# Attention scores of the batch after next put between the turns and the outputs, with the early tiles, query turns and columns' sums reordered

## The chip, the cores and the metric

The kernel runs on one core of one Trainium2 chip. The metric is the device time of one execution in microseconds (us); the number before is the median of 3 runs. A matmul runs on TensorE (PE in the rows), element-wise work on VectorE (DVE), ScalarE (ACT) and GpSimd (POOL); SyncE (SP) issues the loads.

## What is computed

The reference is one block of a first kind, followed by a block of two layers of a second kind, on 512 tokens of width 1024, batch 1, in float32. Cut to what matters here:

```python
# first block: mixer (retention + sparse attention), then a gated feed-forward
h = x + rms_norm(concat([retention(...), dsa_attention(...)]) @ w_out, g_post)
h = h + rms_norm(swiglu_conv(rms_norm(h, g)) @ w_down, g_post)
# second block, layer 0: gated linear attention; layer 1: attention over shared keys
mods = einsum('bd,lde->lbe', silu(c), ada_w) + ada_b      # shift, scale, gate per layer and part
x = x + gate * mixer(rms_norm_2(x, g) * (1 + scale) + shift)
x = x + gate * swiglu(rms_norm_2(x, g) * (1 + scale) + shift, w_in, w_out)
# attention in both blocks: softmax(scale * q @ k.T + mask) @ v, 64 wide per head, tokens in 4 blocks of 128
```

The first block's attention (name `dsa`) has 32 units, one for each of 4 token blocks and 8 heads. The second block's (name `nsa`) has 128 units: 4 token blocks, 16 heads, 2 branches. A unit of token block t reads (t+1)*128 keys, so its rows are n = 128, 256, 384 or 512 wide. `dsa` goes from narrow to wide, `nsa` from wide to narrow. Ahead of `nsa` there is a small attention over 31 compressed keys (`cmp`).

## The kernel before

Each engine has one hand-written program, and semaphores tie them together. An engine takes its instructions strictly in the order in which they are written, so a wait holds everything that stands behind it. Results of TensorE land in the 8 banks of PSUM (`ps`). `open_bank(key)` makes TensorE wait until the last reader of the bank has freed it, `filled(engine, key)` makes a reader wait for the result, `evacuated(engine, key)` waits until it was read. The banks are given out by a plan that runs before the programs are written (`plan_bank`, `plan_attention`).

**Attention** (`attention` of the TensorE program, L2446, with `att_scores`, L2436) goes in batches of four units. For a batch there are these steps: *scores* (L2443, four products q*k into banks 0 to 3, unit i into bank i%4, in two pairs); on VectorE the *logits* (L1770, `logit`: reads the score bank, adds the mask, finds the largest; this frees the bank); on ScalarE the *exponential* (L1134); on TensorE the *turns* (L2461, 128x128 transposes into banks 4 to 6); *copies* of the turned tiles to SBUF, for widths over 256 by ScalarE for even units (L1167) and by VectorE for odd ones (L1794), for the narrow widths two units at a time (L1164, L1791); on TensorE the *outputs* (L2487, bank 7). After every second batch TensorE also turns the finished outputs back (L2472, the key "B"). In step j TensorE does the scores of batch j, the turns of batch j-1, B where due, the outputs of batch j-1.

VectorE's program for step j (`attention` of the VectorE part) is: logits of units 4j, 4j+1, 4j+2; the copies of the turned units 4j-3 and 4j-1 of batch j-1; the logit of unit 4j+3; then `finish` where due. The change leaves this order as it is.

**Norms.** `norm(i)` on TensorE turns the normalised rows of x, one token tile t at a time, into 8 banks ("xT", i, kt). `keep_busy` puts in transposes of the identity whose result nobody reads; `BUSY` says how many stand ahead of each tile. ScalarE (L1014, L1016) and VectorE then read the banks. Ahead of norm(2) and norm(4) TensorE makes the *columns' sums*: `ada_sums`, L2368, sums over partitions of 2 and 4 accumulated rows of `mods`, four one-column products each, with 4 `keep_busy` ahead of each group. They land in a bank of their own, and VectorE's `ada_columns` (L1626, L1636) makes shifts and gains of them.

**Output products.** `out_parts` and the loop over `out_weight` split each piece of the output weight into a high part (ScalarE, L1028) and a low part (VectorE, L1651). `FIRST_HALF_AFTER` says after which piece the first half of which token tiles is added to x (`first_half`: L1509, L1515 on VectorE, L912, L915 on ScalarE).

**Compressed attention.** `PREP` is the order of TensorE's steps: `cmp_first`, `cmp_second` (products of the compression), `cmp_turn` (L2771, the compressed keys turned), `q_turn` (L2783, the queries turned, eight chunks of two parts), `cmp_scores` (L2794).

Of the kernel before, what the change touches and what calls it, by code (L numbers as in the profile page):

```python
# [30 lines left out]
P = 128  # L31
S = 512
NT = S // P
# [57 lines left out]
def build(nc, io, out):  # L91
    ctx = ExitStack()
    with ctx:
# [60 lines left out]
        def carve(sizes):  # L154
# [17 lines left out]
            acc_half zero_done keys_zero k_shifted rk_shifted x0_hi x0_split kv_staged x4_hi x4_split out_hi cmp_zero ret_halved cpt_ready cmp_den kc_copied ones_in_place x_ready_v""".split()  # L172
# [154 lines left out]
        def plan_ffn(i, w_up, w_down):  # L327
            for u in range(FFN_UNITS):
                for j in range(4):
                    plan_bank(("up", i, u, j))  # L330
                for q in range(4):
                    plan_piece(("up", i, u, q), ("up", i, u, 3) if q == 3 else None)
                unit(("up", i, u), together(columns(w_up, u * 256, 256, 0, 512), columns(w_up, DFF + u * 256, 256, 256, 512)),
                     ("sem", "lo_done", splits[0]), ("sem", "lo_done", splits[0] - 2))
                for m, j in ada_after.get((i, u), []):
                    ada_unit(m, j)
                for m, j in ada_after.get((i, u - 1), []):
                    plan_bank(("ada", m, j))
            for m, j in ada_after.get((i, FFN_UNITS - 1), []):
                plan_bank(("ada", m, j))  # L340
            for j in range(8):
                plan_bank(("down", i, j))
            for g, (k0, n) in enumerate(down_groups):
                for k in range(k0, k0 + n):
                    plan_piece(("down", i, k), ("down", i, 7) if k == FT - 1 else None)
                n //= 2
                halves = [[(lambda sl, n=n, h=h: in_halves(sl, n, D)[:, h],
                            w_down[(k0 + h * n) * P:(k0 + h * n + n) * P, :].rearrange("(k p) n -> p k n", p=P))] for h in range(2)]
                unit(("down", i, g), halves, ("sem", "lo_done", splits[0]), ("sem", "lo_done", splits[0] - n))
                for mj in ada_down.get(i, [])[g:g + 1]:  # L350
                    ada_unit(*mj)
            if i in ada_down:
                plan_bank(("ada_columns", i))
# [385 lines left out]
        FIRST_HALF_AFTER = {5: (0, 1, 2), 6: (3,)}  # L739
# [139 lines left out]
        def _(act):  # L879
# [525 lines left out]
        def _(dve):  # L1405
# [79 lines left out]
            def post_norm(stage):  # L1485
# [4 lines left out]
                for t in range(NT):  # L1490
# [3 lines left out]
                    if stage == 1 and t or t == 1:  # L1494
                        x_normed(i, t - 1)
                if stage == 1:
                    ada_columns(0)
                for t in range(NT - 1 if stage == 1 else 1, NT):
                    x_normed(i, t)
# [29 lines left out]
            def post_gate(stage, m):  # L1529
# [4 lines left out]
                for t in range(NT):  # L1534
# [8 lines left out]
                    if t and stage < 5:  # L1543
                        x_normed(i, t - 1)
                if stage == 3:
                    ada_columns(1)
                if stage < 5:
                    x_normed(i, NT - 1)
# [63 lines left out]
            def ada_columns(i):  # L1612

                p = filled(dve, ("ada_columns", i))
                after()
                for n, (m, j) in enumerate(ada_down[i]):
                    ada_column(m, j, p[:, 4 * n:4 * n + 4], free(("ada_columns", i)) if n + 1 == len(ada_down[i]) else None)
                evacuated(dve, ("ada_columns", i))
# [653 lines left out]
        def _(pe):  # L2272
# [33 lines left out]
            BUSY = {0: (15, 0, 0, 0), 1: (0, 26, 0, 0), 2: (0, 12, 8, 4), 3: (0, 0, 0, 0), 4: (0, 0, 0, 0), 5: (0, 0, 0, 0)}  # L2306

            def norm(i):
# [62 lines left out]
            def ffn(i):  # L2371
# [56 lines left out]
                if i in ada_down:  # L2428
                    b = open_bank(("ada_columns", i))
                    for n, mj in enumerate(ada_down[i]):  # L2430
                        pe.wait_ge(s["acc_done"], ADA_N[mj] + 1)
                        keep_busy(b, 4, 1)
                        ins = ada_sums(*mj, b, 4 * n)
                    ins.then_inc(full(("ada_columns", i)), 1)
# [339 lines left out]
            def q_turn(i):  # L2774

                for n, src in enumerate((n_a, n_o)):
# [4 lines left out]
                    b = open_bank(("nT", i, n))  # L2781
# [16 lines left out]
            for what in PREP:  # L2798
                if what == ("q", 7):
                    for i in range(2):  # L2800
                        cmp_scores(i)
                if what[0] == "cmp1":
                    cmp_first(what[1], what[2])
                elif what[0] == "q":
# [3 lines left out]
                else:  # L2808
                    cmp_turn()
# [60 lines left out]
```

## Time and profile before

| | us |
|---|---|
| median of 3 runs | 2098.54 |
| lowest and highest | 2097.39, 2099.53 |
| profiled execution | 2100.61 |
| its span, first to last instruction | 2098.8 |
| TensorE busy in it | 2050.4 (98%) |
| mean granted clock of TensorE | 0.994 |

Between the span and the profiled execution's own time lie 1.8 us, which no instruction fills. Durations in a trace are those of one execution. A matmul's row shows more than its share of the engine, since matmuls overlap: the next row's start less this row's start is what it costs TensorE. So the text works with differences of starts. "PEclk" is the granted clock: 1.00 is 2.4 GHz, 0.50 is 1.2 GHz.

### The profile page before, as it was taken

The page shows a single profiled execution, that of the slowest core. Times are in us where ns is not written, and L with a number is a line of the kernel's source. Part 1 is how long each engine was busy: PE and PEld are TensorE (multiplying, and loading weights), DVE is VectorE, ACT ScalarE, POOL GpSimd, SP SyncE. Part 2 cuts the span into 40 slices and gives each one's busy share as a digit, 9 for nine tenths or more (in the row PEclk, how much of TensorE's full clock was granted, in tenths as well). Part 3 has the DMA queues.
Part 4 walks back from the last instruction along what each step waited for, and adds up shares of the span by engine and source line. Part 5 has one row for each costly group of instructions (what it writes and reads, how often), then busy time and mean ns, then how long its engine had stood idle before and what let it go on. Part 6 is the DMA issues. An engine that isn't in the chain of part 4 may idle for free.

```text
span 2098.8 us, 31247 instructions
## 1 busy us (share of the span) xinstructions
PE 2050.4 (98%) x12283; PEld 1685.7 (80%) x12283; DVE 1245.7 (59%) x2193; ACT 799.0 (38%) x1460; POOL 90.1 (4%) x108
## 2 busy tenths in 40 slices
PE   8999999999999999999999999999899999999999
PEld 7687688888888877787888888879867778888887
DVE  5578667777745449656555545576777755322334
ACT  4323643333424552244222232333557743222222
POOL 1024100000000002000000000001001100000000
PEclk9999999999999999999999999999999999999999
DMA  6221025655433232203655645322300025233321
GB/s 212 81 81 61 21 91 183 198 181 176 161 134 101 81 101 64 81 24 102 206 181 172 203 147 169 123 72 93 124 2 2 2 81 181 81 100 101 100 91 51
DMA packets 146701, 231.51 MB, mean 110 GB/s; under 512 B 7325, under 2 KB 83709, under 8 KB 146557
## 3 DMA queue, kind: packets, MB, share of 16 engines
q1 hardware_dynamic: 144300, 224.05, 32.9%
q0 software_dynamic: 864, 3.15, 0.5%
q8 instruction: 99, 1.62, 0.3%
q10 hardware_dynamic: 1392, 2.33, 0.3%
q14 instruction: 46, 0.37, 0.1%
HBM read 227.41 MB, written 2.10 MB: 109 GB/s over the span
## 4 chain that ended last, share of the span: by engine, by line
PE 86%; DVE 7%; ACT 3%; issue 2%; DMA 0%; POOL 0%; DVEq 0%; ACTq 0%; SPq 0%
PE ps L2393 11%; PE ps L2394 11%; PE ps L2395 11%; PE ps L2421 5%; PE ps L2423 5%; PE ps L2422 5%; PE ps L2654 4%; PE ps L2345 4%; PE ps L2347 4%; PE ps L2346 4%; PE ps L2652 3%; PE ps L2727 3%; PE ps L2487 2%; PE ps L2443 2%; PE ps L2461 2%
## 5 line engine op out<-in xcount | busy, mean ns | idle before, releaser
L1651 DVE TENSOR_TENSOR w_lo<-ring,w_hi 128x1024 fp32r<-128x1024 f32 (+4 forms) x362 | 376.7, 1043 | 662.6 <-ACT w_hi L1028 660.6
L1028 ACT ACTIVATE w_hi<-ring 128x1024 fp32r<-128x1024 f32 (+4 forms) x362 | 328.8, 912 | 916.4 <-PE ps L2395 467.1
L2393 PE MATMUL ps<-x_hi,w_hi 128*128 128x512 f32 x1056 | 415.9, 394 | 0.0
L2395 PE MATMUL ps<-x_hi,w_lo 128*128 128x512 f32 x1056 | 411.2, 389 | 0.0
L2394 PE MATMUL ps<-x_lo,w_hi 128*128 128x512 f32 x1056 | 410.9, 389 | 0.0
L2393 PEld LDWEIGHTS ps<-x_hi,w_hi 128*128 128x128 f32 x1056 | 198.3, 188 | 42.5 <-issue 1.9
L2394 PEld LDWEIGHTS ps<-x_lo,w_hi 128*128 128x128 f32 x1056 | 198.3, 188 | 42.4 <-issue 1.9
L2395 PEld LDWEIGHTS ps<-x_hi,w_lo 128*128 128x128 f32 x1056 | 198.2, 188 | 41.7
L2421 PE MATMUL ps<-w_hi,x_hi 128*128 128x512 f32 x480 | 187.6, 391 | 2.1 <-DVE x_hi L1728 2.1
L2423 PE MATMUL ps<-w_hi,x_hi 128*128 128x512 f32 x480 | 186.8, 389 | 0.0
L2422 PE MATMUL ps<-w_lo,x_hi 128*128 128x512 f32 x480 | 186.8, 389 | 0.0
L2345 PE MATMUL ps<-w_hi,x_hi 128*128 128x512 f32 (+1 forms) x416 | 162.6, 391 | 4.5 <-DVE w_lo L1651 3.8
L2347 PE MATMUL ps<-w_hi,x_lo 128*128 128x512 f32 (+1 forms) x416 | 158.8, 382 | 0.0
L2346 PE MATMUL ps<-w_lo,x_hi 128*128 128x512 f32 (+1 forms) x416 | 158.4, 381 | 0.0
L1592 DVE SCALAR_TENSOR_TENSOR ada_acc<-ring,c_act,ada_acc 128x512 f32<-128x512 f32 x154 | 115.7, 751 | 16.8 <-DVE ada_acc L1592 0.9
L2421 PEld LDWEIGHTS ps<-w_hi,x_hi 128*128 128x128 f32 x480 | 90.1, 188 | 23.6 <-DVE w_lo L1651 5.2
L2423 PEld LDWEIGHTS ps<-w_hi,x_hi 128*128 128x128 f32 x480 | 90.1, 188 | 18.9
L2422 PEld LDWEIGHTS ps<-w_lo,x_hi 128*128 128x128 f32 x480 | 90.1, 188 | 18.3
L2345 PEld LDWEIGHTS ps<-w_hi,x_hi 128*128 128x128 f32 x416 | 78.3, 188 | 26.5 <-issue 8.4
L1134 ACT ACTIVATE arena<-arena,stat 128x128 f32<-128x128 f32 (+3 forms) x160 | 88.0, 554 | 23.1 <-DVE stat L1770 15.6
L2347 PEld LDWEIGHTS ps<-w_hi,x_lo 128*128 128x128 f32 x416 | 78.2, 188 | 15.5
L2346 PEld LDWEIGHTS ps<-w_lo,x_hi 128*128 128x128 f32 x416 | 78.4, 188 | 13.9
(351 smaller groups left out, 3016.0 us busy)
## 6 DMA issues: line engine op xcount, KB each, us to landing
ring<-in_ada_w SPq DMA_DIRECT2D x48, 1024.0 KB, 5.2
ring<-in_ffn_w_in SPq DMA_DIRECT2D x88, 512.0 KB, 4.6
ring<-in_w_up SPq DMA_DIRECT2D x44, 512.0 KB, 4.7
ring<-in_ffn_w_out SPq DMA_DIRECT2D x20, 1024.0 KB, 4.9
ring<-in_hgrn_w_in SPq DMA_DIRECT2D x16, 1024.0 KB, 5.2
ring<-in_w_in SPq DMA_DIRECT2D x12, 1024.0 KB, 5.1
ring<-in_w_down SPq DMA_DIRECT2D x10, 1024.0 KB, 5.0
ring<-in_kv_ada_w SPq DMA_DIRECT2D x8, 1024.0 KB, 5.1
```

The costliest lines, as they stand in the source:

```text
L1028: a.activation(to[:, n % depth, 0:src.shape[-1]], src, ACT.Copy).then_inc(s["hi_done"], 1)
L1592: ins = v.scalar_tensor_tensor(acc, w[:, k], c_act[:, k:k + 1], acc, ALU.mult, ALU.add)
L1651: v.tensor_tensor(to[:, n % depth, 0:width], src, hi[:, n % depth, 0:width].bitcast(F32), ALU.subtract).then_inc(s["lo_done"], 1)
L2345: mm(b, x_hi[:, 2 * q + k, c], hi[:, k], start=((q, k) == (0, 0)), stop=False)
L2346: mm(b, x_hi[:, 2 * q + k, c], lo[:, k], start=False, stop=False)
L2347: ins = mm(b, xl[:, 2 * q + k, c], hi[:, k], start=False, stop=((q, k) == (3, 1)))
L2393: mm(bs[j], wh[:, k, c], x_hi[:, 2 * q + k], start=first, stop=False)
L2394: mm(bs[j], wh[:, k, c], x_lo[:, 2 * q + k], start=False, stop=False)
L2395: ins = mm(bs[j], wl[:, k, c], x_hi[:, 2 * q + k], start=False, stop=last)
L2421: mm(b, hh[:, c], wh[:, f], start=(k == 0), stop=False)
L2422: mm(b, hh[:, c], wl[:, f], start=False, stop=False)
L2423: ins = mm(b, hl[:, c], wh[:, f], start=False, stop=(k == FT - 1))
```

## The change

In the TensorE program of both attentions, the scores of batch j+1 are issued in step j, after the turns of batch j-1 and ahead of B and of the outputs of batch j-1. Scores thus run two batches ahead of the outputs; the four score banks and VectorE's order stay.

```diff
                 for j in range(n_units // 4 + 2):
-                    if j >= ahead:
-                        att_scores(name, j)
+                    if j == 0 and not ahead:
+                        att_scores(name, 0)
                     for i in range(4 * j - 4, 4 * j):
...
                                 ins.then_inc(full(key), 1)
+                    att_scores(name, j + 1)
                     if j >= 3 and j % 2:
```

TensorE in `nsa`, its first batches (512 wide), before: scores are L2443, turns L2461, B L2472, outputs L2487.

```order
L2443 MATMUL ps<-arena 128x512 x4
L2461 MATMUL ps<-small,arena 128x128 x16
L2487 MATMUL ps<-arena 64x128 x16
L2443 MATMUL ps<-arena 128x512 x4
L2461 MATMUL ps<-small,arena 128x128 x16
L2487 MATMUL ps<-arena 64x128 x16
L2443 MATMUL ps<-arena 128x512 x4
L2461 MATMUL ps<-small,arena 128x128 x16
L2472 MATMUL ps<-small,arena 128x128 x4
L2487 MATMUL ps<-arena 64x128 x16
```

The same place after: scores are L2449, turns L2467, B L2479, outputs L2494.

```order
L2449 MATMUL ps<-arena 128x512 x4
L2467 MATMUL ps<-small,arena 128x128 x16
L2449 MATMUL ps<-arena 128x512 x4
L2494 MATMUL ps<-arena 64x128 x16
L2467 MATMUL ps<-small,arena 128x128 x16
L2449 MATMUL ps<-arena 128x512 x4
L2494 MATMUL ps<-arena 64x128 x16
L2467 MATMUL ps<-small,arena 128x128 x16
L2449 MATMUL ps<-arena 128x512 x4
L2479 MATMUL ps<-small,arena 128x128 x4
L2494 MATMUL ps<-arena 64x128 x16
```

Each group of scores moved ahead of the outputs (and of B) that it stood behind.

The columns' sums move from the end of the feed-forward into norm(2) and norm(4), ahead of the last token tile, with 2 instead of 4 `keep_busy` a group, and land in the last tile's place of the last bank; the last turn there waits until VectorE has read them. VectorE does the last `x_normed` ahead of `ada_columns`, and in stage 3 each `x_normed` one step earlier. `BUSY` of norm(2) goes from (0, 12, 8, 4) to (0, 12, 4, 0).

```diff
@@ norm(i) of TensorE
                 for t in range(2, NT):
+                    held = i // 2 - 1 if t == NT - 1 and i in (2, 4) else None
+                    if held is not None:
+                        for n, mj in enumerate(ada_down[held]):
+                            pe.wait_ge(s["acc_done"], ADA_N[mj] + 1)
+                            keep_busy(banks[0], 2, t)
+                            ins = ada_sums(*mj, banks[KT - 1], t * P + 4 * n)
+                        ins.then_inc(s["columns_in"], 1)
                     keep_busy(banks[0], BUSY[i][t], t)
                     pe.wait_ge(s["xn_ready"], NT * i + t + 1)
-                    tiles(t, range(KT))
+                    tiles(t, range(KT - 1))
+                    if held is not None:
+                        pe.wait_ge(s["columns_out"], held + 1)
+                    tiles(t, (KT - 1,))
@@ post_gate of VectorE
                         gated(stage, m, 0, t)
+                        if t and stage < 5:
+                            x_normed(i, t - 1)
                         gated(stage, m, 1, t)
```

TensorE between the last product of the second feed-forward and the first product of the next stage, before (sums are L2368, `keep_busy` L2279, tiles L2314):

```order
L2279 MATMUL ps<-small 128x128 x4
L2368 MATMUL ps<-ones,arena 128x1 x4
L2279 MATMUL ps<-small 128x128 x4
L2368 MATMUL ps<-ones,arena 128x1 x4
L2279 MATMUL ps<-small 128x128 x4
L2368 MATMUL ps<-ones,arena 128x1 x4
L2279 MATMUL ps<-small 128x128 x4
L2368 MATMUL ps<-ones,arena 128x1 x4
L2314 MATMUL ps<-small,arena 128x128 x32
L2279 MATMUL ps<-small 128x128 x12
```

and after (sums are L2381, `keep_busy` L2282, tiles L2317):

```order
L2317 MATMUL ps<-small,arena 128x128 x24
L2282 MATMUL ps<-small 128x128 x2
L2381 MATMUL ps<-ones,arena 128x1 x4
L2282 MATMUL ps<-small 128x128 x2
L2381 MATMUL ps<-ones,arena 128x1 x4
L2282 MATMUL ps<-small 128x128 x2
L2381 MATMUL ps<-ones,arena 128x1 x4
L2282 MATMUL ps<-small 128x128 x2
L2381 MATMUL ps<-ones,arena 128x1 x4
L2317 MATMUL ps<-small,arena 128x128 x8
L2282 MATMUL ps<-small 128x128 x12
```

24 of the 32 tiles moved ahead of the sums, and 8 `keep_busy` are gone.

The last query turns stand in another order among the compressed attention's steps, with 14 `keep_busy`. Before (query turns L2783, compressed keys turned L2771, scores L2794):

```order
L2762 MATMUL ps<-arena,small 31x64 x16
L2783 MATMUL ps<-small,arena 128x128 x8
L2771 MATMUL ps<-small 128x31 x2
L2783 MATMUL ps<-small,arena 128x128 x8
L2794 MATMUL ps<-small,h_t 128x128 x8
L2783 MATMUL ps<-small,arena 128x128 x8
```

and after (query turns L2792, keys L2778, scores L2803, `keep_busy` L2282):

```order
L2769 MATMUL ps<-arena,small 31x64 x16
L2792 MATMUL ps<-small,arena 128x128 x12
L2282 MATMUL ps<-small 128x128 x12
L2792 MATMUL ps<-small,arena 128x128 x4
L2282 MATMUL ps<-small 128x128 x2
L2792 MATMUL ps<-small,arena 128x128 x4
L2778 MATMUL ps<-small 128x31 x2
L2803 MATMUL ps<-small,h_t 128x128 x4
L2792 MATMUL ps<-small,arena 128x128 x4
L2803 MATMUL ps<-small,h_t 128x128 x4
```

Three of the four last parts of the query turns now stand ahead of the keys' turn or of the scores.

Two tables change: the first half of the last token tile is added after weight piece 7 instead of 6, and ScalarE reads the four retention outputs in the order 0, 1, 3, 2.

```diff
-        FIRST_HALF_AFTER = {5: (0, 1, 2), 6: (3,)}
+        FIRST_HALF_AFTER = {5: (0, 1, 2), 7: (3,)}
...
-                    t = i - 3
+                    t = (0, 1, 3, 2)[i - 3]
```

## Rows read from the trace of the kernel before

**Rows 1.** Window `nsa`: length; busy PE, PEld, DVE, ACT, POOL; PEclk, DMA share, GB/s.

```profile
1537.80:1678.80 141.00, 134.82 (x1289) 97.72 (x1290) 102.87 (x358) 100.57 (x316) 19.05 (x15) 1.00 0.01 2
```

**Rows 2.** Waits in `nsa`: us in total, times, longest.

```profile
DVE arena L1770 <- PE ps L2443: 25.8, 23, 1.7
```

**Rows 3.** Timeline of TensorE, 512 wide: start, length, instruction, count, [idle before].

```profile
1563.73 1.99 PE L2443 MATMUL ps<-arena 64*128 64x512 f32 x8
...
1567.60 0.64 PE L2472 MATMUL ps<-small,arena 128*128 128x128 f32 x4
1568.18 1.97 PE L2487 MATMUL ps<-arena 128*64 128x128 f32 x32
1570.07 1.99 PE L2443 MATMUL ps<-arena 64*128 64x512 f32 x8
1571.99 2.12 PE L2461 MATMUL ps<-small,arena 128*128 128x128 f32 x16
1574.04 2.11 PE L2487 MATMUL ps<-arena 128*64 128x128 f32 x32
1576.08 0.70 PE L2443 MATMUL ps<-arena 64*128 64x512 f32 x2
```

**Rows 4.** Timeline of VectorE in the same batch: the last copy, the last logit.

```profile
1574.22 0.69 DVE L1794 COPY arena<-ps 128x512 f32<-128x512 f32 x1 [0.34 <-PE ps L2461]
1574.83 0.68 DVE L1770 CUSTOM_DVE_ANT_0 arena<-ps,small 128x512 f32<-128x512 f32 x1
```

**Rows 5.** Timeline, start of `nsa`: scores that wait for logits.

```profile
1537.82 1.13 PE L2443 MATMUL ps<-arena 64*128 64x512 f32 x4 [0.78 <-DVE stat L1770]
...
1536.98 0.68 DVE L1770 CUSTOM_DVE_ANT_0 arena<-ps,small 128x512 f32<-128x512 f32 x1
```

**Rows 6.** Timelines of TensorE and VectorE, 256 wide.

```profile
1638.78 1.14 PE L2443 MATMUL ps<-arena 64*128 64x256 f32 x8
1639.85 1.09 PE L2461 MATMUL ps<-small,arena 128*128 128x128 f32 x8
1641.34 1.20 PE L2487 MATMUL ps<-arena 128*64 128x128 f32 x16 [0.40 <-ACT arena L1164]
1642.47 1.13 PE L2443 MATMUL ps<-arena 64*128 64x256 f32 x8
...
1646.16 1.13 PE L2443 MATMUL ps<-arena 64*128 64x256 f32 x8
...
1641.04 0.69 DVE L1791 COPY arena<-ps 128x512 f32<-128x512 f32 x1 [0.41 <-PE ps L2461]
1641.65 0.41 DVE L1770 CUSTOM_DVE_ANT_0 arena<-ps,small 128x256 f32<-128x256 f32 x1
```

**Rows 7.** Timeline of VectorE in `dsa`: a logit that waits for scores.

```profile
207.29 0.42 DVE L1770 CUSTOM_DVE_ANT_0 arena<-ps,arena 128x256 f32<-128x256 f32 x1 [1.96 <-issue]
```

**Rows 8.** Norm(4): timeline of TensorE, of ScalarE, and a window.

```profile
1350.76 0.60 PE L2279 MATMUL ps<-small 128*128 128x128 f32 x4
...
1356.94 5.91 PE L2314 MATMUL ps<-small,arena 128*128 128x128 f32 x32
...
1362.18 0.78 ACT L1014 ACTIVATE ada_acc<-ps,mod 128x512 f32<-128x512 f32 x1 [7.91 <-PE ps L2314]
...
1354.70:1361.50 6.80, 6.80 (x35) 6.80 (x34) 1.43 (x8) 0.00 (x0) 0.00 (x0) 0.50 0.20 72
```

**Rows 9.** Compressed attention: timelines of TensorE and ScalarE, and a window.

```profile
1507.33 0.31 PE L2771 MATMUL ps<-small 31*128 31x31 f32 x2 [4.00 <-DVE small L2195]
...
1509.71 3.78 PE L2794 MATMUL ps<-small,h_t 128*128 128x128 f32 x16 [0.81 <-DVE small L2203]
...
1515.73 0.70 ACT L1386 ACTIVATE arena<-arena 128x248 f32<-128x248 f32 x2
...
1508.30:1515.10 6.80, 5.99 (x28) 5.28 (x26) 3.77 (x10) 1.97 (x4) 0.00 (x0) 0.50 0.00 0
```

**Rows 10.** Output product of layer 1: TensorE waits for the low part of piece 7.

```profile
1717.95 0.50 PE L2345 MATMUL ps<-w_hi,x_hi 128*128 128x512 f32 x1 [0.93 <-DVE w_lo L1651]
```

More of the change, by code:

```diff
@@ L171, in build @@
             tables_done whole_done hi_done lo_done piece_done x_split hid_hi acc_done gate_row_in0 gate_row_in1
-            acc_half zero_done keys_zero k_shifted rk_shifted x0_hi x0_split kv_staged x4_hi x4_split out_hi cmp_zero ret_halved cpt_ready cmp_den kc_copied ones_in_place x_ready_v""".split()
+            acc_half zero_done keys_zero k_shifted rk_shifted x0_hi x0_split kv_staged x4_hi x4_split out_hi cmp_zero ret_halved cpt_ready columns_in columns_out cmp_den kc_copied ones_in_place x_ready_v""".split()
         s = {n: sem(n) for n in names}
@@ L352, in plan_ffn @@
             if i in ada_down:
-                plan_bank(("ada_columns", i))
+                turn[0] = (turn[0] + 1) % 8
         def plan_out(name, w, n_in=KT):
@@ L1495, in post_norm @@
                         x_normed(i, t - 1)
+                for t in range(NT - 1 if stage == 1 else 1, NT):
+                    x_normed(i, t)
                 if stage == 1:
                     ada_columns(0)
-                for t in range(NT - 1 if stage == 1 else 1, NT):
-                    x_normed(i, t)
                 if i != 2:
@@ L1542, in post_gate @@
                         gated_added(stage, 1, t)
-                    if t and stage < 5:
+                    if t and stage in HALF_FIRST:
                         x_normed(i, t - 1)
+                if stage < 5:
+                    x_normed(i, NT - 1)
                 if stage == 3:
                     ada_columns(1)
-                if stage < 5:
-                    x_normed(i, NT - 1)
                 if i in (3, 5):
@@ L1612, in ada_columns @@
             def ada_columns(i):
-                p = filled(dve, ("ada_columns", i))
+                dve.wait_ge(s["columns_in"], i + 1)
+                p = ps[:, bank_use["xT", 2 * i + 2, KT - 1][0], (NT - 1) * P:]
                 after()
                 for n, (m, j) in enumerate(ada_down[i]):
-                    ada_column(m, j, p[:, 4 * n:4 * n + 4], free(("ada_columns", i)) if n + 1 == len(ada_down[i]) else None)
-                evacuated(dve, ("ada_columns", i))
+                    ada_column(m, j, p[:, 4 * n:4 * n + 4], s["columns_out"] if n + 1 == len(ada_down[i]) else None)
+                dve.wait_ge(s["columns_out"], i + 1)
                 after()
@@ L2304, in turn @@
                 ins.then_inc(full(key), 1)
-            BUSY = {0: (15, 0, 0, 0), 1: (0, 26, 0, 0), 2: (0, 12, 8, 4), 3: (0, 0, 0, 0), 4: (0, 0, 0, 0), 5: (0, 0, 0, 0)}
+            BUSY = {0: (15, 0, 0, 0), 1: (0, 26, 0, 0), 2: (0, 12, 4, 0), 3: (0, 0, 0, 0), 4: (0, 0, 0, 0), 5: (0, 0, 0, 0)}
             def norm(i):
@@ L2427, in ffn @@
                         ins.then_inc(s["piece_done"], 1)
[L2428 to L2434, printed above, removed]
             def att_scores(name, j):
@@ L2772, in cmp_turn, with q_turn @@
                 ins.then_inc(full("cmpT"), 1)
-            def q_turn(i):
-                for n, src in enumerate((n_a, n_o)):
+            def q_turn(i, parts=(0, 1), idle=0):
+                for n in parts:
+                    b = open_bank(("nT", i, n))
+                    keep_busy(b, idle)
                     if n == 0:
@@ L2780, in q_turn @@
                         pe.wait_ge(s["rope2_done"], NT + i + 1)
-                    b = open_bank(("nT", i, n))
+                    src = (n_a, n_o)[n]
                     for c in range(4):
@@ L2798, in _ @@
             for what in PREP:
-                if what == ("q", 7):
-                    for i in range(2):
-                        cmp_scores(i)
                 if what[0] == "cmp1":
                     cmp_first(what[1], what[2])
-                elif what[0] == "q":
+                elif what[0] == "q" and what[1] < 6:
                     q_turn(what[1])
@@ L2807, in _ @@
                     cmp_second()
-                else:
-                    cmp_turn()
+            q_turn(6, (0,))
+            q_turn(6, (1,), 12)
+            q_turn(7, (0,), 2)
+            cmp_turn()
+            cmp_scores(0)
+            q_turn(7, (1,))
+            cmp_scores(1)
             for t in range(NT):
```

## The prediction

> **What bounds the kernel now.** TensorE is busy for 98% of the span, so I looked first for the few places where it is not, in the windows around the edits, and then for what is late there, in the timelines and the waits. In the 141.0 us of `nsa` TensorE is busy for 134.82 at a granted clock of 1.00 [rows 1]. So at most 6.2 us of it could be won there by a better order, whatever the other engines wait. The most visible wait of the stage is another one: VectorE's logits wait 25.8 us for scores [rows 2]. The moved scores aim at that, but VectorE is busy only 102.87 of the 141.0 us [rows 1]; its waiting costs nothing as long as TensorE works. What counts is what TensorE will wait for in the new order.
>
> **The scores, 512 wide.** Before, a batch without B takes from one start of scores to the next 1570.07 to 1576.08 = 6.01 us: scores 1.92, turns 2.05, outputs 2.04; one with B takes 1563.73 to 1570.07 = 6.34, with .58 for B and 1.89 for the outputs behind it [rows 3]. TensorE doesn't wait in either.
>
> In the new order the scores of batch j+1 stand right behind the turns of batch j-1. Their second pair writes banks 2 and 3, and bank 3 is free only when logit 4j+3 has read it. VectorE does that logit behind the copies of batch j-1 (units 4j-3 and 4j-1), and its order is not changed; the copies need the very turns that have just been made. Before, the outputs of 2.04 us stood between the turns and the next scores and covered copy and logit. Now nothing covers them. The way from the start of the turns to the second pair is, in rows: to the last copy 1571.99 to 1574.22 = 2.23, copy to logit .61, the logit .68 [rows 3, 4], and from its end to the score matmul that it releases .16 (1536.98 + .68 to 1537.82, where just such a wait is seen) [rows 5]. Sum 3.68. Behind it come the second pair, half of 1.92 = .96, and the outputs, 2.04: 6.68 against 6.01, +.67. With B the outputs are 1.89 and B adds its .58: 7.11 against 6.34, +.77. The mean is +.72 a batch. The first pair (.96) fits into the wait: turns 2.05 + .96 = 3.01 is below 3.68.
>
> **Narrower batches.** 256 wide a batch takes 3.69, with B (1642.47 to 1646.16) or without (1638.78 to 1642.47), since without B the outputs wait .40 for a copy by ScalarE, and with B it fills that time [rows 6]. New: turns to copy 1639.85 to 1641.04 = 1.19, copy to logit .61, logit .41 [rows 6], release .16 [rows 5]: 2.37; second pair, half of 1.07, .53; outputs 1.13: 4.03, +.34. With B .58 more, as at 512: 4.61, +.92. Mean +.63. The wait of the outputs is gone in this sum, since the scores cover it, but a longer one stands ahead of the scores. For 384 I take between the two, +.68. For 128 I have no complete cycle in rows; I carry the fall from .72 to .63 on to +.50. With 7, 8, 8 and 7 batches that have both a successor and a predecessor: 5.0 + 5.4 + 5.0 + 3.5 = **+18.9**. If each batch also wins back .15, because the scores' data are there earlier for ScalarE, it is 14.4; if release and copy cost .1 more each time, 21.9.
>
> Here a rule of the Trainium skill bears on the row. By "Perfetto Trace Analysis", section "Matmuls" under "Optimizing Tensor Performance", independent groups of matmuls should rotate through different PSUM banks, so that the reading out of one overlaps the next group. The change asks four score banks to serve two batches ahead, which speaks against it; it gives no price, and the sum above is from rows alone.
>
> **The scores in `dsa`.** It goes from narrow to wide in only eight batches. A wait of VectorE's logit of 1.96 [rows 7] should go, and TensorE can win at most about that; three wide batches lose some .7 each as above. I take 0, and keep -3 to +3.
>
> **Columns' sums and norm(4).** Before, TensorE makes the sums from 1350.76, the 32 tiles start only at 1356.94, and ScalarE's first reading of the finished banks is at 1362.18; the clock is .50 from 1354.7 to 1361.5 [rows 8]. After, 24 tiles start in place of the sums (32 take 5.2 at the slow clock, so 24 take 2.0 to 3.9), then sums with half of the `keep_busy`, then 8 tiles. All the tensor work is still there but for 8 `keep_busy` of .15 (four take .60 in the row), 1.2 us; what is new is that the tiles run while the clock is still up: 24 tiles at 1.00 instead of .50 save 2.0. Sum -3.2. The last turn now waits for VectorE's reading of the sums, some .7, hidden only if the last turns of the other banks cover it (7 turns of .16 at the slow clock, 1.1; of .08 at the fast, .6). If the clock falls again in the tiles, -1.0 is left. I take -2.8, range -3.2 to -1. VectorE's earlier `x_normed` stands ahead of the last `gated` of a tile, which comes some .3 later; it is read later still, so 0. **Norm(2)** has the same move with 8 `keep_busy` fewer, but it waits for the rows of the last token tile: -.5, range -1.2 to -.2.
>
> **Compressed attention.** TensorE idles 4.00 us ahead of the keys' turn at 1507.33; then the clock is .50 from 1508.3 to 1515.1 [rows 9]. In this stretch stand both first scores (1509.71, sixteen matmuls, 3.57 us) and then the last query turns. ScalarE copies these turned queries ahead of its first exponential, which starts at 1515.73 [rows 9]. After, one part of the last chunk is turned ahead of the first score and the other between the two; the idle 4.00 us holds most of the moved work. The first score still starts at about 1509.7, since it needs VectorE's copy of the keys. It and its half of the turns take 1.8 + .6 at the slow clock; the exponential can start when VectorE has subtracted the maxima, some 1.5 behind the score: 1513.1, gain 2.6; at the full clock 1512.2, gain 3.5. I take -2.8, range -3.6 to -1.5.
>
> **Weight piece 7.** TensorE waits .93 for the low part of the last piece, since ScalarE squares the first half of the last token tile ahead of the high part [rows 10]. With the half after piece 7 this goes; by differences of starts the stall costs 1.1. The same wait stands in the first layer's output product and not in the first block's, so 2 x 1.1 = -2.2; the half itself comes later and is covered by the products of piece 7, or costs a part again: range -2.2 to -1. **The order 0, 1, 3, 2** of the retention outputs: what waits for the third is behind the second pair of scores anyway, 0.
>
> **Sum:** 18.9 + 0 - 2.8 - .5 - 2.8 - 2.2 = +10.6. Against the profiled execution of 2100.61 that is 2111.2; that one lies 2.07 above the median of 2098.54, so against the median 2109.1. Low end of the costs: 14.4 - 3 - 3.2 - 1.2 - 3.6 - 2.2 = +1.2, 2099.7. High end: 21.9 + 3 - 1 - .2 - 1.5 - 1 = +21.2, 2119.7; both ends at once are unlikely.
>
> **Rivals.**
> A, the forecast: the second pair is held by logit 4j+3 in every batch. For it: program order and banks, both of which the change leaves, and the 3.68 in rows. 2109.1, chance .66.
> B, faster: the second pair is not held, because the logit ends within .96 of the turns' end. Then the waits of the outputs for copies go as well (.40 without B at 256), up to the 6.2 that TensorE idles [rows 1]. The time is then 2098.5 - 8.3 - 0 to 6.2 = 2084 to 2090. It decides at 2.05 + .96 = 3.01 from the start of the turns, where the rows give 3.68; the copy would have to be .67 earlier. Against it: the copy waits only .34 for TensorE in [rows 4], and can't start before the turns end. Chance .08.
> C, held half as long: the copy goes as soon as its unit is turned, VectorE arrives earlier since its logits wait less, and a batch loses .35. 18.9 becomes 9.4: +1.1, 2099.6. For it: VectorE's 25.8 us of waits go and it has time to spare. Against it: the last copy hangs on the last turn, not on VectorE. Chance .15.
> D, the clock falls in `nsa` too. With the new waits TensorE idles in each narrow batch, and where it idled 4.00 us the clock then stood at .50 for 6.8 us [rows 9], which costs 3.4 of work. Two to three such windows in the 128-wide batches add 7 to 10: 2116 to 2119. Against it: the clock is 1.00 throughout `nsa` now [rows 1], with waits of .40 in every other batch. Chance .11.
> The Trainium skill, "Perfetto Trace Analysis", section "Matmul Optimizations", says that the matmul engine scales power with its utilization and that matmuls should run back-to-back; that is the side of D, and this trace shows it where TensorE had idled 4.00 us.
>
> **How the numbers follow.** About .2% (2094.3 to 2102.7) is what a measurement of this kernel can tell from no change. B is faster, .08. C lies within .2% mostly (.11), partly slower (.04). A and D are slower but for A's lower tail (.05 within .2%). So faster .08, same .16, slower .76. The range leaves out B and the far end of D: 2098.5 to 2117.5.
>
> **What would show it.** In `nsa` a batch at 512 takes about 6.7 and 7.1 in place of 6.01 and 6.34, the second pair of scores has an idle of some .6 that ends with logit, and the whole of `nsa` is some 19 us longer with TensorE's busy time unchanged. VectorE's waits for scores become waits for turned tiles (its copies). Norm(4)'s first reading by ScalarE is at 1359.4 or earlier by the old count, the first exponential of the compressed attention 2.8 earlier, and no wait of .93 stands at piece 7. Were the second pair not to wait, the prediction would be wrong by its largest term; were the wait ended by copies of ScalarE instead, the mechanism would be wrong though the sign might hold.

## The result and the profile after

The changed kernel takes 2120.61 us (median of 4 runs, 2116.43 to 2122.69) where the one before takes 2098.76: the ratio is 1.0108, interval 1.0096 to 1.0120, or +20 to +25 us. The forecast was slower, +10.6, and 2109.1; the measured time lies above its range, which ended at 2117.5. The profiled execution of the changed kernel took 2122.69 us; the sums below go by it, against the profiled 2100.61 of before.

How far each stage of the trace of after lies behind that of before, read at the same instruction in both, gives the change of each stage:

| stage | forecast | trace of after | that edit alone, timed |
|---|---|---|---|
| moved scores in `nsa` | +18.9 | +20.1 | +20.5 (17.6 to 23.5) |
| moved scores and the retention order in `dsa` | 0 | +3.1 | scores +0.7 (difference of two runs), order -2.3 |
| norm(2) | -0.5 | -0.4 | both norms |
| norm(4) | -2.8 | +2.8 | +0.6 (-1.3 to +2.5) |
| compressed attention | -2.8 | -2.0 | -1.0 (-2.9 to +0.8) |
| weight piece 7, two times | -2.2 | -2.2 | -2.1 (-4.0 to -0.2) |
| between | 0 | +0.8 | |
| sum | +10.6 | +22.2 | |

"Between" is -0.8 from 750 to 924 us, which kernels that change nothing there (e10_ret and others) show too, and +1.6 at 930, where the granted clock was .50 for 3.4 us in this execution. It is no work of the change.

**The scores.** The window over `nsa` of the changed kernel (columns as in [rows 1]), and the waits in it:

```profile
1540.90:1702.20 161.30, 141.29 (x1290) 96.81 (x1291) 102.26 (x359) 101.62 (x316) 19.12 (x15) 1.00 0.01 2
```

```profile
DVE arena L1797 <- PE ps L2467: 26.0, 32, 2.3
...
PE ps L2449 <- DVE stat L1773: 19.1, 32, 1.4
```

161.3 us where [rows 1] has 141.0, at the same clock of 1.00. The scores (now L2449) wait 32 times for a logit (now L1773), once a batch and 19.1 us in all; before there were two such waits, both at the start of `nsa`, of 2.2 us together. The busy time of TensorE didn't stay as it was, as the prediction had it: by the rows it rose from 134.82 to 141.29 with the same instructions (1289 and 1290). A group that a wait splits is two rows, and each row shows more than its share: 1.13 + 1.13 for the eight score matmuls that were 1.99 in one row. So the idle time in the rows (.49 a batch) is less than the batch loses, and the differences of starts have to be used. VectorE's wait for scores, 25.8 in [rows 2], isn't gone but has another name: it now waits 26.0 for turned tiles (L2467) ahead of its copies. A wait of an engine with time to spare was exchanged for another one of the same engine, and TensorE pays.

One batch at 512 wide, TensorE and then VectorE (answers to [rows 3] and [rows 4]):

```profile
1566.93 1.13 PE L2449 MATMUL ps<-arena 64*128 64x512 f32 x4
...
1573.56 1.13 PE L2449 MATMUL ps<-arena 64*128 64x512 f32 x4
1575.18 1.13 PE L2449 MATMUL ps<-arena 64*128 64x512 f32 x4 [0.49 <-DVE stat L1773]
1576.24 0.66 PE L2479 MATMUL ps<-small,arena 128*128 128x128 f32 x4
1576.83 1.97 PE L2494 MATMUL ps<-arena 128*64 128x128 f32 x32
1578.73 2.12 PE L2467 MATMUL ps<-small,arena 128*128 128x128 f32 x16
1580.78 0.70 PE L2449 MATMUL ps<-arena 64*128 64x512 f32 x2
```

```profile
1573.74 0.69 DVE L1797 COPY arena<-ps 128x512 f32<-128x512 f32 x1 [0.34 <-PE ps L2467]
1574.35 0.68 DVE L1773 CUSTOM_DVE_ANT_0 arena<-ps,small 128x512 f32<-128x512 f32 x1
```

The first pair goes at once (1573.56), the second at 1575.18, which is .15 after the logit that began at 1574.35 has ended. The batch takes 1573.56 to 1580.78 = 7.22 with B; the one ahead of it, without B, takes 1566.93 to 1573.56 = 6.63. At 256 wide (answer to [rows 6]):

```profile
1653.21 0.70 PE L2449 MATMUL ps<-arena 64*128 64x256 f32 x4
...
1657.83 0.70 PE L2449 MATMUL ps<-arena 64*128 64x256 f32 x4
1659.18 0.70 PE L2449 MATMUL ps<-arena 64*128 64x256 f32 x4 [0.65 <-DVE stat L1773]
1659.81 1.09 PE L2494 MATMUL ps<-arena 128*64 128x128 f32 x16
1660.84 1.09 PE L2467 MATMUL ps<-small,arena 128*128 128x128 f32 x8
1661.86 0.49 PE L2449 MATMUL ps<-arena 64*128 64x256 f32 x2
```

1657.83 to 1661.86 is 4.03 us, where before it was 3.69; with B, from 1653.21, it is 4.62. The waits of the outputs for a copy ([rows 6] show one), nine in `nsa` with 4.1 us before, are down to one of .5.

**Norm(4).** TensorE; VectorE's last read of a product bank (a bank that still holds a result of the feed-forward) and ScalarE's first of a finished one; a window (answers to [rows 8]):

```profile
1353.11 1.03 PE L2317 MATMUL ps<-small,arena 128*128 128x128 f32 x8
1356.34 2.52 PE L2317 MATMUL ps<-small,arena 128*128 128x128 f32 x16 [2.19 <-DVE arena L1509]
1358.66 0.63 PE L2282 MATMUL ps<-small 128*128 128x128 f32 x2
1359.09 1.71 PE L2381 MATMUL ps<-ones,arena 128*128 128x1 f32 x8
...
1366.73 1.95 PE L2317 MATMUL ps<-small,arena 128*128 128x128 f32 x8
...
1355.41 0.68 DVE L1509 TENSOR_TENSOR arena<-ps,row 128x512 f32<-128x512 f32 x1
...
1367.29 0.78 ACT L1014 ACTIVATE ada_acc<-ps,mod 128x512 f32<-128x512 f32 x1 [8.58 <-PE ps L2317]
...
1357.50:1371.20 13.70, 13.59 (x68) 13.20 (x66) 4.19 (x13) 5.09 (x10) 0.53 (x1) 0.50 0.10 38
```

8 tiles start where the sums had stood, then TensorE waits 2.19 us, and what it waits for is not rows of x but a bank: L1509 on VectorE reads the last product of the feed-forward out of it. The clock is .50 for 13.7 us, from 1357.5, and the four groups of sums take 8.07 (1358.66 to 1366.73) where they took 6.18 before.

**Compressed attention.** ScalarE's first exponential; TensorE's first score (answers to [rows 9]):

```profile
1518.31 0.41 ACT L1386 ACTIVATE arena<-arena 128x248 f32<-128x248 f32 x1
...
1514.85 2.07 PE L2803 MATMUL ps<-small,h_t 128*128 128x128 f32 x8 [1.82 <-DVE small L2206]
```

This kernel is 5.12 us behind before ahead of that place, so the score starts where it did and the exponential 2.5 us earlier. No wait for a low part of piece 7, as in [rows 10], is left.

### The profile page after: what moved, and what is told of

Same layout as the page of the kernel before. It is cut to its first block, busy times and chain, and to the rows that moved or that the text cites. A ratio compares the mean times of both kernels' runs of the same rounds, so it can differ in the third digit from the quotient of the medians.

```text
span 2120.9 us, 31231 instructions
## 1 busy us (share of the span) xinstructions
PE 2059.2 (97%) x12277; PEld 1687.4 (80%) x12277; DVE 1245.1 (59%) x2193; ACT 800.9 (38%) x1460; POOL 90.1 (4%) x108
## 4 chain that ended last, share of the span: by engine, by line
PE 86%; DVE 7%; issue 3%; ACT 3%; DMA 0%; POOL 0%; DVEq 0%; ACTq 0%; SPq 0%
PE ps L2406 11%; PE ps L2408 11%; PE ps L2407 11%; PE ps L2434 4%; PE ps L2358 4%; PE ps L2661 4%; PE ps L2436 4%; PE ps L2435 4%; PE ps L2360 4%; PE ps L2359 4%; PE ps L2659 3%; PE ps L2734 3%; PE ps L2467 2%; PE ps L2494 2%; PE ps L2449 2%
## 5 line engine op out<-in xcount | busy, mean ns | idle before, releaser
L1594 DVE SCALAR_TENSOR_TENSOR ada_acc<-ring,c_act,ada_acc 128x512 f32<-128x512 f32 x154 | 115.8, 752 | 16.8 <-DVE ada_acc L1594 0.9
L2435 PEld LDWEIGHTS ps<-w_lo,x_hi 128*128 128x128 f32 x480 | 90.1, 188 | 18.5
L2449 PE MATMUL ps<-arena 64*128 64x128 f32 (+3 forms) x320 | 65.4, 485 | 27.3 <-DVE stat L1773 26.8
```

Of the source, the lines that this page charges most:

```text
L1594: ins = v.scalar_tensor_tensor(acc, w[:, k], c_act[:, k:k + 1], acc, ALU.mult, ALU.add)
L2435: mm(b, hh[:, c], wl[:, f], start=False, stop=False)
```

## Experiments

Each ratio is against the kernel before on the same chip and in the same series; the signed number behind it is that ratio on 2098, in us. An interval of a ratio that is .0010 wide to each side is 2.1 us to each side.

### Is it VectorE's order that holds the scores?

**e1_scores**: the score diff alone.

> The kernel before with the moved scores alone, in both attentions. Theory H (the second pair of scores waits for logit 4j+3, which stands on VectorE behind the copies of the turns just made): nsa 20 us longer with 6.6 and 7.2 us a batch at 512 wide, and dsa some 3 longer, as in the trace of the changed kernel: 2121 to 2123. Rival C2 (the edits interact: a lower clock that the other edits bring makes part of it): nsa less than 17 longer here, below 2117.

2120.16, ratio 1.0101 (1.0087 to 1.0114), +21.2. Its trace has +20.1 in `nsa` and +1.4 in `dsa`. The moved scores carry the whole loss by themselves.

**e4_logit_first**: e1_scores and, on VectorE,

```diff
                     for i in range(4 * j, 4 * j + 3):
                         logits(i)
+                    logits(4 * j + 3)
                     if 1 <= j <= n_units // 4:
                         turned(4 * j - 3)
                         turned(4 * j - 1)
-                    logits(4 * j + 3)
```

> The kernel before with the moved scores, and on VectorE logit 4j+3 ahead of the copies of the turns (one edit more than e1_scores). Theory H: bank 3 is free long before the second pair, the wait of .7 to 1 us a batch goes; at 512 wide a batch is back at 6.0 and 6.35, at 256 below 3.69 since outputs no longer wait for copies, nsa 135 to 139 us instead of 141: 2092 to 2098. Rival S (what holds the scores is the banks of the turns or ScalarE's copies, not VectorE's order): little changes against e1_scores, 2115 to 2122.

2093.14, ratio 0.9972 (0.9962 to 0.9983), -5.9: 27 us better than e1_scores by the place of one instruction in each step. TensorE at 512 wide, and the window over `nsa`:

```profile
1560.31 1.99 PE L2443 MATMUL ps<-arena 64*128 64x512 f32 x8
1562.23 1.97 PE L2488 MATMUL ps<-arena 128*64 128x128 f32 x32
1564.12 2.12 PE L2461 MATMUL ps<-small,arena 128*128 128x128 f32 x16
1566.17 1.99 PE L2443 MATMUL ps<-arena 64*128 64x512 f32 x8
```

```profile
1535.00:1673.20 138.20, 135.18 (x1288) 98.41 (x1289) 102.51 (x358) 101.06 (x316) 19.15 (x15) 0.99 0.01 2
```

All eight score matmuls stand in one row again, with no idle: the batch is 1560.31 to 1566.17 = 5.86 us, below the 6.01 of before. Rival S is out: had ScalarE or the turns' banks held the scores, this edit would not have freed them. 138.2 us for `nsa` is the kind of gain that rival B of the prediction described, under the condition that it named as missing.

**e12_logit_only**: that edit without the moved scores, the control.

> The kernel before with logit 4j+3 ahead of the copies on VectorE and the scores where they were: the control of e4_logit_first. Theory H: the order of VectorE matters only where scores run two batches ahead; alone it makes the copies later by one logit (.4 to .7 us), so no gain: 0 to +6 us, that is, the 5.8 us of e4_logit_first come from both edits together. Rival L: the logit ahead is a gain by itself, 3 us or more faster than before.

2111.63, ratio 1.0068 (1.0054 to 1.0082), +14.3, more than I expected. At 512 wide, TensorE, then VectorE:

```profile
1572.92 2.12 PE L2461 MATMUL ps<-small,arena 128*128 128x128 f32 x16
1575.35 0.66 PE L2472 MATMUL ps<-small,arena 128*128 128x128 f32 x4 [0.31 <-DVE arena L1794]
```

```profile
1574.00 0.69 DVE L1770 CUSTOM_DVE_ANT_0 arena<-ps,small 128x512 f32<-128x512 f32 x1
...
1574.61 1.28 DVE L1794 COPY arena<-ps 128x512 f32<-128x512 f32 x2
```

Here the fourth logit (1574.00) delays both copies, and TensorE waits for the copies behind the turns: .31 ahead of B, and .40 ahead of the outputs in the next batch, which has no B. A batch takes 6.34 for 6.01, with B 6.84 for 6.34. By the trace 5.2 us of it are in `nsa` and 8.3 in `dsa`; in `dsa` the clock was .50 for 13.6 us in this execution and for 10.2 in that of before. So each of the two orders alone is a loss and both together are a gain.

**e17_nsa_scores**: e1_scores with `dsa` as before.

> The kernel before with the moved scores in nsa alone. Of the +21.2 of e1_scores its trace puts 20.1 into nsa and 1.4 into dsa, so +20: 2117 to 2119 where before is 2097 to 2099. If dsa carries more than the trace of one execution shows, it is below +18.

2117.82, ratio 1.0098 (1.0084 to 1.0112), +20.5. So `dsa` carries .7 of the 21.2, too little to be told from 0 by time. The traces say more, if those are compared in which the clock was .50 in `dsa` for equally long. With 10.2 us of it the old score order stays within .3 us of before (e9_w7, e17_nsa_scores), while the moved scores with the new retention order are 1.9, 1.9 and 3.0 us longer over the stage (e6_after_again, e18_after_no_norms, the changed kernel). With 6.8 us it is -1.3 and -0.4 (e15_four_busy, e3_norms) against +1.3 and +1.7 (e1_scores, e19_after_ret_old). So by the traces the scores cost some 2 us in `dsa` too.

### What are the other edits worth?

**e2_rest**: the changed kernel without the score diff.

> The changed kernel with the scores back where they were, so all the other edits together. The prediction's sum for them was -8.3: 2090.5. The trace of the changed kernel gives -0.4 (norm 2) +2.75 (norm 4) -2.0 (compressed attention) -2.2 (piece 7 twice) and +0.9 in between, about -1: 2098. A time near 2098 says that norm(4) loses what the other edits gain, whatever the scores do.

2094.19, ratio 0.9980 (0.9971 to 0.9989), -4.2: less than the forecast of -8.3, more than the trace of after let me expect.

**e9_w7**: `FIRST_HALF_AFTER = {5: (0, 1, 2), 7: (3,)}` alone.

> The kernel before with the first half of the last token tile after weight piece 7 and nothing else. By the prediction -2.2, 1.1 in each of the second block's two output products: 2096.8. Rival: a first block that loses what these gain (the half comes later there too), within .5 of before.

2094.53, ratio 0.9990 (0.9981 to 0.9999), -2.1, the forecast's -2.2.

**e10_ret**: `t = (0, 1, 3, 2)[i - 3]` alone.

> The kernel before with the order 0, 1, 3, 2 of the retention outputs alone. The prediction gave it 0, since with moved scores the outputs behind it wait for something else. The profiles show 2.0 us less in dsa where it stands beside the old score order (e2_rest against e3_norms) and nothing beside the new one (e7_after_logit_first against e4_logit_first). So here -2: 2095 to 2097 where before is 2097 to 2099. Rival: that difference is the clock's, then 0.

2095.31, ratio 0.9989 (0.9981 to 0.9998), -2.3. In rows, the first outputs of `dsa`: in the kernel before, in e2_rest (this order, old scores), and in the changed kernel the second pair of scores that now stands ahead of them:

```profile
204.88 1.12 PE L2487 MATMUL ps<-arena 128*64 128x128 f32 x8 [2.20 <-ACT arena L1219]
```

```profile
203.81 0.77 PE L2493 MATMUL ps<-arena 128*64 128x128 f32 x8 [0.99 <-DVE arena L1794]
```

```profile
204.97 0.70 PE L2449 MATMUL ps<-arena 64*128 64x256 f32 x4 [1.55 <-DVE stat L1773]
```

The order takes 1.1 us off a wait; the moved scores put 1.55 in its place. The other 1.2 of the 2.3 no row shows, and the interval (-4.0 to -0.4) doesn't ask for them.

**e11_cmp**: the query turns alone.

> The kernel before with the order of the last query turns alone. Prediction -2.8; the profiles of the changed kernel show -2.0 between 1500 and 1520; the timings of the parts leave -1.0 for it (-4.8 less 0.2, -2.0 and -2.0). Between -2.8 and -1.

2097.31, ratio 0.9995 (0.9986 to 1.0004), -1.0, not to be told from 0. In its trace the stage is 1.3 us shorter, and 1.5 us are lost again at 1536.8, where the clock was .50 for 3.4 us; it was 1.00 there in before.

### Why does norm(4) not gain?

**e3_norms**: the move of the columns' sums with all that belongs to it.

> The kernel before with the move of the columns' sums alone (norms 2 and 4, the earlier x_normed, fewer keep_busy). By the prediction -3.3: 2095.5. By the trace of the changed kernel +2.4 to +3.2: 2101 to 2102, with a wait of TensorE of about 2.2 us for x_normed(2) between the 8 and the 16 tiles of norm(4) and the four groups of sums at 2.0 us each at half clock.

2099.2, ratio 1.0003 (0.9994 to 1.0012), +0.6. TensorE and VectorE in norm(4):

```profile
1349.78 1.03 PE L2317 MATMUL ps<-small,arena 128*128 128x128 f32 x8
1353.01 1.94 PE L2317 MATMUL ps<-small,arena 128*128 128x128 f32 x16 [2.20 <-DVE arena L1509]
1354.79 0.38 PE L2282 MATMUL ps<-small 128*128 128x128 f32 x2
1355.00 0.95 PE L2381 MATMUL ps<-ones,arena 128*128 128x1 f32 x8
1355.82 0.42 PE L2282 MATMUL ps<-small 128*128 128x128 f32 x2
```

```profile
1352.08 0.68 DVE L1509 TENSOR_TENSOR arena<-ps,row 128x512 f32<-128x512 f32 x1
```

The wait is the same. But the group of sums takes 1.03 us here and 2.02 in the changed kernel's execution: the clock fell in another place. Half of my expectation (2.0 a group) was taken from one execution, and was wrong.

**e8_norm_filled** (`BUSY[4] = (0, 0, 20, 0)`) and **e13_sums_in_wait** (the sums ahead of token tile 2) were meant to fill the 2.2 us.

> e3_norms with 20 keep_busy in the 2.2 us in which TensorE waits for x_normed(2) in norm(4). Theory K (the idle stretch is what lets the clock fall among the sums): the groups of sums all take 1.05 us, the last turns run at full clock, ScalarE's first reading comes 1 to 2 us earlier than in e3_norms: 2097 to 2098. Rival N (the sums themselves, one-column products, let it fall whatever stands ahead): clock and time as e3_norms, 2099, or some .3 more.

> e3_norms with the columns' sums of norms 2 and 4 one token tile earlier: ahead of the tiles of token tile 2, where TensorE waits 2.2 us for x_normed(2), and the last bank's tile 2 turned with its tile 3. If that wait is what the prediction missed in norm(4), the sums fill it: some 2 us less than e3_norms at the same clock. Rival N: the clock falls earlier, since the sums start earlier, and takes it back: as e3_norms.

2100.4, ratio 1.0020 (1.0011 to 1.0029), +4.2, and 2100.89, ratio 1.0010 (1.0001 to 1.0019), +2.1. Neither filled it: both traces have the same wait (2.18 and 2.20 us) and the added work behind it. I had taken the wait for one on x_normed(2), which stands ahead of tile 2; it is the wait for the upper four banks, which stands earlier. The two misses led to reading the releaser, L1509.

**e14_xn_old**: e3_norms with the `x_normed` of stage 3 back behind the last `gated`:

```diff
                         gated(stage, m, 0, t)
-                        if t and stage < 5:
-                            x_normed(i, t - 1)
                         gated(stage, m, 1, t)
...
-                    if t and stage in HALF_FIRST:
+                    if t and stage < 5:
                         x_normed(i, t - 1)
```

> e3_norms with the x_normed of stage 3 back behind the last gated of its token tile. Theory P (the earlier x_normed holds the last read of the product banks, and TensorE waits 2.2 us for that bank): the wait between the first 8 tiles and the rest goes, a shorter one of about 1.1 for x_normed(2) takes its place, and norm(4) is 1.1 shorter than in e3_norms at the same clock. Rival Q (the wait of 2.2 is for x_normed(2) itself): the 16 tiles start later than in e3_norms, by .6.

TensorE, and the VectorE instruction it now waits for:

```profile
1349.09 2.24 PE L2315 MATMUL ps<-small,arena 128*128 128x128 f32 x16
1352.10 1.09 PE L2315 MATMUL ps<-small,arena 128*128 128x128 f32 x8 [0.77 <-DVE arena L1418]
```

```profile
1351.29 0.76 DVE L1418 TENSOR_SCALAR arena<-x_tok,stat 128x1024 f32<-128x1024 f32 x1
```

16 tiles go at once, then a wait of .77 for x_normed(2). From the first tile to the first `keep_busy` of the sums (1353.03) it is 3.94 us, in e3_norms 5.01: the 1.1 that theory P asks, at a clock of 1.00 in both. Rival Q is out. By time it is 2095.85, ratio 0.9996 (0.9988 to 1.0005): 1.4 below e3_norms, though the intervals overlap.

**e15_four_busy**: e14_xn_old with `keep_busy(banks[0], 4, t)`.

> e14_xn_old with 4 keep_busy ahead of each group of sums as before the change, 12 instructions more in all (4 groups of norm 4, 2 of norm 2), .7 us at full clock. Theory K2 (fewer keep_busy let the clock fall for longer): the mean granted clock goes up by .001 or more and the time down by 1 us or more. Rival: the clock as in e14_xn_old, time +.7.

2097.14, ratio 1.0002 (0.9993 to 1.0011), +0.4; the mean granted clock of the timed runs is .9955 in both. Four `keep_busy` in place of two gave back no clock that these runs show.

**Norm(4) over all traces.** The length from TensorE's first instruction behind the last product to ScalarE's first reading (L1014), and how long the clock was .50 in it (labels shortened to their numbers):

| order | traces | length, us | at .50, us | length less half of that |
|---|---|---|---|---|
| before | before, e1, e4, e11, e16, e17 | 11.4 | 6.8 | 8.0 |
| before | e9, e10, e12, e18 | 8.1 | 0 | 8.1 |
| changed | changed kernel | 14.2 | 9.8 | 9.3 |
| changed | e6, e19, e2 | 11.8 to 12.2 | 4.8 to 5.5 | 9.4 |
| changed | e7, e3 | 10.3, 10.4 | 1.7, 1.8 | 9.5 |
| x_normed put back | e14 | 8.6 | 0 | 8.6 |
| the same, 4 `keep_busy` a group | e15 | 9.4 | 0 | 9.4 |

One of the second line, e10_ret, TensorE and then ScalarE:

```profile
1347.77 0.60 PE L2279 MATMUL ps<-small 128*128 128x128 f32 x4
...
1355.89 0.78 ACT L1014 ACTIVATE ada_acc<-ps,mod 128x512 f32<-128x512 f32 x1 [4.61 <-PE ps L2314]
```

Taking off half of the stretch at .50 brings the two forms of the old order within .1 us of each other, so the last column can be compared. The old order alone takes 8.1 or 11.4 us, by the clock, and the one trace that the forecast was read from had the long form. Brought to one clock, the changed order is 1.4 us longer than the old one, not shorter. Putting `x_normed` back takes .9 of that away and leaves .5; the eight further `keep_busy` of e15_four_busy cost .9. So of the +2.7 of the changed kernel's trace about 1.3 is the order, and 1.5 that the clock was .50 for 2.9 us longer.

### Do the parts add up?

**e6_after_again** and **e7_after_logit_first** (the changed kernel; the same with the logit first):

> The changed kernel once more, beside the two runs that take it apart. If the parts add up (scores +21.2, the rest -4.8) it is at 2115.4. If the first runs of it (2120.6, 2116.4 to 2122.7) hold, some 5 us come from the parts together; by the profiles that would be norm(4), whose sums ran at half clock for all of their 8 us with the scores moved and at full clock for three groups of four without, so a matter of when the clock falls.

> The changed kernel with logit 4j+3 ahead of the copies on VectorE, one edit. Theory H with parts that add up: 2093.1 - 4.8 = 2088.3, faster than both kernels; nsa about 138 us. If the retention order and the moved scores both take the same wait in dsa, up to 2 us less gain: 2090.

2117.62, ratio 1.0100 (1.0086 to 1.0114), and 2090.89, ratio 0.9975 (0.9965 to 0.9985). The four small edits alone sum to -4.8 (0.6 - 2.1 - 2.3 - 1.0), as e2_rest (-4.2) says. But beside the moved scores nothing of it shows in the times: e6_after_again is within .2 of e1_scores, and e7_after_logit_first within .7 of e4_logit_first, where each such difference has room for some 2 to 3 us. Piece 7 is not what got lost: its 1.1 stands twice in each of the traces of the changed kernel, e6, e7, e18 and e19.

**e18_after_no_norms** and **e19_after_ret_old**: the changed kernel without the edits of the norms, and with the retention order of before.

> The changed kernel without the edits of the norms (columns' sums, x_normed, keep_busy as before). If the norms cost clock beside the moved scores: 2 us or more below the changed kernel, that is +18 to +19.5 against before. If the norms are worth their +0.6 here too: +20.5 to +21.5.

> The changed kernel with the retention outputs read in the order 0, 1, 2, 3. The prediction held that with moved scores this order is worth nothing, since V(0) stands behind the second pair of scores: the same as the changed kernel within 1 us, +20.5 to +22.5. If it keeps its gain of 2.3 there: +23 to +25; if it does harm in dsa (its traces show +2.0 and +3.1 there, +1.4 without the other edits): +20 or less.

1.0096 (1.0079 to 1.0113), +20.1, and 1.0095 (1.0080 to 1.0110), +19.9, where the changed kernel has +21.0 and +22.7. A retention order that kept its 2.3 would have put e19_after_ret_old at +23 or more, the end of its interval (+16.8 to +23.1); so it has probably lost it, as the prediction argued, and the rows of e10_ret show how. Where the other 2 us go isn't settled: each difference lies inside the intervals of some 3 us.

### A version that beats both

**e16_best**: scores moved and logit first in `nsa` only, `dsa` in its old order, the two tables.

> The kernel before with moved scores and the logit ahead of the copies in nsa alone, dsa as before, and the two tables of the change (weight piece 7, order 0, 1, 3, 2); no norms, no query turns. The parts: nsa about -4.8 (e4_logit_first less its -.8 in dsa), piece 7 -2.0, order -2.3: -9, so 2088 to 2090 where before is 2097 to 2099, faster than both kernels.

2088.8 us, ratio 0.9961 (0.9947 to 0.9974), -8.2. The window over `nsa`:

```profile
1533.50:1670.00 136.50, 133.40 (x1286) 97.10 (x1287) 102.19 (x359) 100.89 (x315) 19.15 (x15) 1.00 0.01 2
```

136.5 us against 141.0, with 3.1 of idle TensorE left of 6.2.

## Why the prediction was wrong in size and right in kind

- **The hold of the second pair: right, with its price.** Forecast 6.68 and 7.11 us a batch at 512, measured 6.63 and 7.22; at 256 4.03 and 4.61, measured 4.03 and 4.62. The stage is +20.1 for +18.9. e1_scores, e4_logit_first and e12_logit_only together show the cause. For the +10.6 of the forecast the trace has +22.2; of the 11.6 that are missing this term has 1.2, norm(4) 5.6, `dsa` 3.1, the compressed attention .8, norm(2) .1, and .8 is no work of the change.
- **"VectorE's earlier `x_normed` stands ahead of the last `gated` of a tile, which comes some .3 later; it is read later still, so 0": the step that failed.** The last `gated` (L1509) starts at 1355.41, and 2.36 us of that are from earlier stages: 1353.05, where before it started at 1350.96. So it came 2.1 later, since `x_normed(2)` first waits .85 for ScalarE's root and then takes .9 itself. And nobody had to read the result for it to cost: this instruction frees a bank that TensorE's tiles write. I followed its output and not its input. With it fell "24 tiles start in place of the sums": 8 did, and TensorE idled 2.19 us. At one clock this hold is worth .9 to 1.1 us (e14_xn_old against e3_norms).
- **Norm(4)'s clock: mis-sized.** -2.8 took 2.0 us from tiles that would run at full clock where one trace had them at .50. That stretch isn't a cost of the old order: four of its ten traces are without it. And the changed order had its own, with sums at 2.02 us a group in one execution and 1.03 in another. Forecast -2.8, timed +0.6 with norm(2) together, +2.8 in the profiled execution, and 1.4 longer at one clock.
- **Norm(2).** It loses 12 `keep_busy` (8 by `BUSY`, 4 ahead of its two groups of sums), where the prediction counted 8; -0.5 was forecast, -0.4 is in the trace.
- **Compressed attention.** The exponential came 2.5 earlier. The prediction had 2.6 for the slow clock and 3.5 for the full one and took 2.8; the clock was .50 from 1514.6 for 3.4 us. The stage's end came 2.0 earlier, the time alone 1.0.
- **`dsa`: mis-sized.** 0 was forecast within -3 to +3; the traces have +1.4 for the scores alone and +2.0 and +3.1 with the other edits, the times .7 for the scores. A new wait of 1.55 us came ahead of the second pair (rows at e10_ret), and the sum had no term for it.
- **Piece 7 and the retention order:** -2.2 and 0 beside moved scores. The first is as measured; the second fits the runs, within their noise. That the order alone would be worth 2.3 the prediction didn't say.
- **The range** ended at 2117.5, while the sum of its high ends was 2119.7. "Both ends at once are unlikely" was given without a reason, and norm(4) and `dsa` both went past their high ends in the trace (+2.8 for -1, +3.1 for +3).
- Rival C is out (a hold half as long), rival B as it stood (it needed the second pair not held), and rival D too (clock 1.00 in `nsa`).

Open stay: where the last 2 us of the small edits go beside the moved scores, and why the clock falls where it does. That the norms' move gains anything in its repaired form isn't shown: e14_xn_old is at -0.8 (-2.5 to +1.0), and its norm(4) at full clock is .5 us longer than that of before.

## To carry to other kernels

When work is put ahead on one engine, look at what the consumer's program has in front of the instruction that frees its buffer; if that waits for the producer's newest work, both orders must be moved together or neither. When an instruction is delayed, ask what its reading frees, not only who uses its result. A wait of an engine that has time to spare is no price, and taking it away is no gain. Before a gain is read from a stretch at half clock, look whether other executions of the same code have that stretch at all.

## Of the hardware, not expected

How long and where the granted clock falls changes between executions by more than most edits here are worth. In one series of 24 timed runs of the kernel before, mean clocks of .994 to .997 go with 2102.03 to 2094.77 us. At norm(4) the clock was .50 for 6.8 us in the trace of before, 13.7 in that of the changed kernel, 3.4 in e14_xn_old (behind ScalarE's first reading) and not at all in e15_four_busy. A stage's difference between two traces that has such a stretch in it, 1 to 3 us, has to be read with the clock beside it, or timed.
